# Four of twelve modulation units moved from the first block's layers to the start of the second block

## What is computed

```python
def first_block(...):
    h = x
    for l in range(DEPTH):                      # 2
        h = h + hybrid_mixer(rmsnorm(h, norm_mix[l]), ...)
        h = h + expert_choice_ffn(rmsnorm(h, norm_ffn[l]), ...)
    return rmsnorm(h, norm_final)

def adaln(cvec, w, b):                          # w: 1024 x 6144
    m = jax.nn.silu(cvec) @ w + b
    return [t[..., None, :] for t in jnp.split(m, 6, axis=-1)]

def second_block(x, c, ctx, c_ctx, ...):
    x = x + sincos_2d(...)
    sh1, sc1, gt1, sh2, sc2, gt2 = adaln(c, ada_w[l], ada_b[l])
    csh1, csc1, cgt1, csh2, csc2, cgt2 = adaln(c_ctx, ada_w[l], ada_b[l])
    ...                                         # the context's states use csh1 and csc1
    hx = modulate(rms_norm(x, norm1_g[l]), sh1, sc1)
    x_mix = token_mixer(hx @ w_in[l], ...)
    x = x + gt1 * x_mix
    x = x + gt2 * hier_moe(modulate(rms_norm(x, norm2_g[l]), sh2, sc2), ...)
```

## Time and profile before

| | us |
|---|---|
| median of 3 runs | 2249.55 |
| lowest, highest | 2248.14, 2252.38 |
| the profiled execution | 2247.0 |
| its span, first to last instruction | 2245.2 |
| PE busy in it | 1932.7 |
| DVE, ACT busy | 660.6, 553.6 |
| moved by DMA | 748.76 MB, mean 333 GB/s |

### The profile page before, as it was taken

The page is one execution under the profiler, slowest core; times in us unless marked ns, Lnnn a source line. Parts: engine busy times, 40 slices in busy tenths (PEclk is TensorE's granted clock), DMA queues, the critical chain, the costliest instruction groups (busy, mean ns, idle before and its releaser), DMA issues.

```text
span 2245.2 us, 29187 instructions
## 1 busy us (share of the span) xinstructions
PE 1932.7 (86%) x12802; PEld 1136.0 (51%) x12802; DVE 660.6 (29%) x1074; ACT 553.6 (25%) x849; POOL 0.2 (0%) x4
## 2 busy tenths in 40 slices
PE   7989998777777998998898988879999988888886
PEld 7977932121221897893223433338889732222222
DVE  3467510000000447750150111036657400000001
ACT  3457310000000345630111221023444311010101
POOL 0000000000000000000000000000000000000000
PEclk9999999999999999998999999999999999999999
DMA  9722799999999963379999999983423999999996
GB/s 363 272 100 99 303 389 422 421 421 422 422 421 420 365 237 122 114 309 376 421 418 413 417 417 417 421 321 113 150 95 135 381 421 422 422 422 422 422 421 273
DMA packets 153247, 748.76 MB, mean 333 GB/s; under 512 B 6064, under 2 KB 18608, under 8 KB 78768
## 3 DMA queue, kind: packets, MB, share of 16 engines
q1 hardware_dynamic: 153136, 747.11, 82.9%
HBM read 746.04 MB, written 1.05 MB: 333 GB/s over the span
## 4 chain that ended last, share of the span: by engine, by line
PE 47%; DMA 34%; SPq 9%; ACT 4%; DVE 4%; issue 2%; DVEq 0%; ACTq 0%
PE bank L724 19%; DMA ring<-w_expert_up 12%; DMA ring<-w_expert_down 11%; SPq L2813 9%; PE bank L790 8%; DMA ring<-moe_w_down 6%; PE bank L727 5%; DMA ring<-w_expert_gate 4%; PE bank L820 4%; PE bank L831 1%; PE bank L751 1%; PE bank L974 1%; PE bank L994 1%; DMA ring<-ada_w 1%; PE bank L735 1%
## 5 line engine op out<-in xcount | busy, mean ns | idle before, releaser
L790 PE MATMUL bank<-ring,arena 128*32 128x512 f32 x2560 | 513.3, 600 | 101.6 <-DMA ring<-w_expert_up 52.0
L820 PE MATMUL bank<-ring,arena 128*32 128x512 f32 x1280 | 284.9, 606 | 81.6 <-DMA ring<-w_expert_down 61.5
L790 PEld LDWEIGHTS bank<-ring,arena 128*32 128x32 f32 x2560 | 127.2, 110 | 444.2 <-issue 267.9
L724 PE MATMUL bank<-arena_parts,ring_parts 128*128 128x256 f32 x1376 | 314.5, 284 | 2.4 <-DVE ring_parts L2458 1.6
L724 PEld LDWEIGHTS bank<-arena_parts,ring_parts 128*128 128x128 f32 x1376 | 233.5, 189 | 11.8 <-issue 3.1
L820 PEld LDWEIGHTS bank<-ring,arena 128*32 128x32 f32 x1280 | 67.9, 111 | 287.4 <-issue 153.5
L1519 ACT ACTIVATE arena<-bank 128x512 f32<-128x512 f32 (+1 forms) x150 | 76.0, 536 | 509.7 <-PE bank L806 244.4
L2040 DVE TENSOR_TENSOR arena<-arena,bank 128x512 f32<-128x512 f32 x24 | 15.8, 686 | 591.2 <-PE bank L790 591.2
L724 PE MATMUL bank<-ring_parts 128*128 128x256 f32 x768 | 151.1, 287 | 11.7 <-DVE ring_parts L2458 5.3
L724 PE MATMUL bank<-hnT_parts,ring_parts 128*128 128x256 f32 x544 | 154.3, 284 | 0.0
L724 PEld LDWEIGHTS bank<-ring_parts 128*128 128x128 f32 x768 | 123.8, 191 | 14.7 <-issue 5.2
(11 more groups left out here) (353 smaller groups left out, 2399.4 us busy)
## 6 DMA issues: line engine op xcount, KB each, us to landing
ring<-w_expert_down SPq DMA_DIRECT2D x64, 2048.0 KB, 26.1
ring<-w_expert_up SPq DMA_DIRECT2D x60, 2048.0 KB, 25.0
ring<-w_expert_gate SPq DMA_DIRECT2D x56, 2048.0 KB, 23.4
ring<-w_in SPq DMA_DIRECT2D x34, 2048.0 KB, 10.9
ring<-moe_w_up SPq DMA_DIRECT2D x24, 2048.0 KB, 29.4
ring<-moe_w_gate SPq DMA_DIRECT2D x20, 2048.0 KB, 32.5
ring<-moe_w_down SPq DMA_DIRECT2D x16, 2048.0 KB, 33.0
arena<-moe_w_down SPq DMA_DIRECT2D x16, 2048.0 KB, 32.4
```

The costliest lines, as they stand in the source:

```text
L724: last = pe.matmul(out[:, n * S:(n + 1) * S], w[:, k, n * P:(n + 1) * P], x[:, k, :], start=first, stop=final)
L790: last = pe.matmul(banks[bank0 + f][32 * e:32 * e + 32, :], x_slots[:, c, 32 * e:32 * e + 32], w[:, k, i, f * 512:(f + 1) * 512], start=c ...
L820: last = pe.matmul(banks[4 + d][32 * e:32 * e + 32, :], hidT[:, f, 32 * e:32 * e + 32], w[:, k, i, d * 512:(d + 1) * 512], start=f == 0, s ...
```

## The change

In each layer the head has four ada units now (`ADA_UNITS = 4`), whose columns are still counted by six (`ADA_SPLIT`). The two that are left out (layer 0: units 4 and 5 of 12, layer 1: 10 and 11, the halves of both gates) form `ADA_LATE`. They are loaded at the passage to the second block, in slots 1 and 2, behind the first `w_in_2` unit and ahead of the second and third. TensorE takes two of them between the sums of squares of `f norm` and `x norm`, and two behind `x norm` in place of the filler; the loads of the latter two wait for the former two. ScalarE copies the four results between its second and third weight split, TensorE turns them behind the first projection, VectorE adds the bias after its third weight split.

In the layers, slots 4 and 5 are free earlier: units 8 and 9 of tile 0 are loaded behind units 1 and 2 (`TILE_ORDER`), as soon as `w_branch_a` has been used, and unit 7 moves ahead of 5 and 6. The slots of all units of tile 0 stay as they are. The second block's counts of loads (`RING_LOADS`, `late_before`) follow, and the position table lies 256 columns lower, because the kept ada values are read longer.

```diff
-ADA_UNITS = 6
+ADA_SPLIT = 6
+ADA_UNITS = 4
+ADA_LATE = [layer * ADA_SPLIT + n for layer in range(LAYERS) for n in range(ADA_UNITS, ADA_SPLIT)]
...
+TILE_ORDER = (1, 2, 8, 9, 3, 4, 7, 5, 6)
...
-HEAD_ORDER = [0, 18, 19, 1, 2, 20, 3, 21] + list(range(4, 18)) + [22, 23]
+HEAD_ORDER = [0, 18, 19, 1, 2, 20, 3, 21] + list(range(4, 18))
...
                 token_rows(1)
                 token_rows(3)
-                for n in range(ADA_HEAD, ADA_UNITS):
-                    ada_unit(n)
...
                 def other_slots():
-                    ada_cols("ada 5", take(6, "dve", "ada 5 cols"), ada_rows_late, ADA_UNITS - ADA_HEAD)
...
             for j in range(4):
                 sum_squares_part("f norm", hn3, j, norm_bank, "f squares")
+            late_bank = take(5, "act", "ada late")
+
+            def ada_late(n):
+
+                at = 1 + n % 2
+                pe.wait_ge(unit_loaded[at], (RING_LOADS[at] + 1 + n // 2) * 16)
+                ada_products(late_bank, at, n).then_inc(pe_done, pe_p.mark(f"ada late {n}"))
+
+            ada_late(0)
+            ada_late(1)
             norm_bank = take(7, "act", "x norm root")
             for j in range(4):
                 sum_squares_part("x norm", hn3, j, norm_bank, "x squares")
-            idle_products(banks[4], 16)
+            ada_late(2)
+            ada_late(3)
...
             for n in range(6):
                 job2(HY0 + n, to_dve(f"hy {n}"), hx_high, hn_low, ready=None if n else hx_ready)
+                if n == 0:
+                    ada_cols("ada late", take(4, "dve", "ada late cols"), ada_rows_late, len(ADA_LATE))
...
-            for i in range(1, 8):
+            high2(1)
+            act.wait_ge(pe_done, pe_at(f"ada late {len(ADA_LATE) - 1}"))
+            act.activation(ada_rows_late, banks[5][:], ACT.Copy).then_inc(act_done, act_p.mark("ada late"))
+            for i in range(2, 8):
                 high2(i)
...
                 sp.wait_ge(pe_done, pe_at(f"o win {WIN_HEADS // 2 - 1}", loops))
-                for u in range(1, RING + SPARE):
+                for u in TILE_ORDER:
                     if u == 7:
                         sp.wait_ge(dve_done, dve_at("yb 3", loops))
                     load_tile_unit(0, u)
...
             for i in range(UNITS2_HEAD):
-                if i < HEAD_SLOTS:
-                    sp.wait_ge(pe_done, pe_at(unit_step(STREAMS[LAYERS - 1][i - RING][0])))
+                if i == 0:
+                    sp.wait_ge(pe_done, pe_at(unit_step(STREAMS[LAYERS - 1][-RING][0])))
+                elif i < HEAD_SLOTS:
+                    sp.wait_ge(pe_done, pe_at(f"ada late {i + 1}"))
...
+                if i == 0:
+                    for n, unit in enumerate(ADA_LATE):
+                        at = 1 + n % 2
+                        step = unit_step(STREAMS[LAYERS - 1][at - RING][0]) if n < 2 else f"ada late {n - 2}"
+                        sp.wait_ge(pe_done, pe_at(step))
+                        load_cols(at, io["ada_w_2"], 512 * unit)
```

More of the change, by code:

```diff
@@ L143, in loads @@
             held[at] = (layer, unit)
-    assert count[:RING] == [RING_LOADS] * RING
-    return nth, prior
-NTH_LOAD, PRIOR = loads()
+    return nth, prior, count
+NTH_LOAD, PRIOR, RING_LOADS = loads()
 def unit_step(unit):
@@ L931, in shift_turned, with ada_cols, ada_products @@
                 last.then_inc(pe_done, pe_p.mark("shift cols"))
+            def ada_cols(step, out, of, n_units):
+                pe.wait_ge(act_done, act_at(step, loops))
+                for n in range(n_units):
+                    last = pe.transpose(out[:, n * P:(n + 1) * P], of[:, n * P:(n + 1) * P], ident)
+                last.then_inc(pe_done, pe_p.mark(f"{step} cols"))
+            def ada_products(bank, at, n):
+                w = slot(at).rearrange("p (k n) -> p k n", k=DC)
+                for k in range(DC):
+                    for b in range(4):
+                        last = pe.matmul(bank[32 * b:32 * b + 32, n * P:(n + 1) * P], c_pairs[:, 2 * k:2 * k + 32],
+                                         w[:, k, b * P:(b + 1) * P], start=k == 0, stop=k == DC - 1)
+                return last
             background = {
@@ L1055, in ada_unit @@
                     u = 18 + n
-                    if n % 4 == 0:
-                        ada_banks[n // 4] = take(7, "act", f"ada {min(n + 3, ADA_UNITS - 1)}")
+                    if n == 0:
+                        ada_banks[0] = take(7, "act", f"ada {ADA_UNITS - 1}")
                     if layer == 0 and n == 0:
@@ L1060, in ada_unit @@
                     unit_ready(("head", u), layer)
[L1061 to L1065, removed]
+                    last = ada_products(ada_banks[0], HEAD_AT[u] % RING, n)
                     last.then_inc(pe_done, pe_p.mark(f"ada {n}", unit_done(u)))
@@ L1073, in _ @@
                     job(i, hn_high, hn_low, hn_ready if i == 0 else None)
[L1075 to L1081, removed]
+                ada_cols("ada 3", to_dve("ada 3 cols"), ada_rows, ADA_UNITS)
                 pe.wait_ge(dve_done, dve_at("k_win", loops))
@@ L1823, in high2 @@
                 unit = JOBS2[i][0]
[L1824 removed]
+                act.wait_ge(*head2_loaded(unit))
                 if i >= 2:
@@ L2309, in ada_cols @@
                        .then_inc(dve_done, dve_p.mark(f"{step} cols"))
-                kept = 4 * ADA_UNITS * layer
-                ada_cols("ada 3", bank_v(), ada_raw[:, kept:kept + 4 * ADA_HEAD, :])
+                kept = 4 * ADA_SPLIT * layer
+                ada_cols("ada 3", bank_v(), ada_raw[:, kept:kept + 4 * ADA_UNITS, :])
                 pairs = WIN_HEADS // 2
@@ L2432, in _ @@
                 diagonal("gate diag", gate_diag, topv)
-                ada_cols("ada 5", banks[6], ada_raw[:, kept + 4 * ADA_HEAD:kept + 4 * ADA_UNITS, :])
                 dve.wait_ge(pe_done, pe_at("slot tokens", loops))
@@ L2512, in _ @@
                 low2(j + 2)
+                if j == 0:
+                    late = 4 * ADA_UNITS
+                    n = 4 * ADA_SPLIT - late
+                    dve.wait_ge(pe_done, pe_at("ada late cols"))
+                    dve.tensor_tensor(ada_by_layer[:, :, late:], banks[4][:].rearrange("p (l n x) -> p l n x", l=LAYERS, n=n)[:, :, :, 0:2],
+                                      ada_bias[:, :, late:].broadcast_to([P, LAYERS, n, 2]), ALU.add)\
+                       .then_inc(dve_done, dve_p.mark("ada late cols"))
                 if j == 3:
```

37 lines of the change are left out of this document (19 added, 18 removed).

## The result

| | median us | runs | against the kernel before |
|---|---|---|---|
| before | 2247.58 | 21 | |
| changed | 2252.22 | 21 | 1.0018, 95% interval 1.0011 to 1.0024 |
| changed, measured again | 2251.81 | 9 | 1.0024, 1.0014 to 1.0034 |

The change costs about 4 us (0.18%, interval 2.5 to 5.4 us). That is a little under the 0.2% which the prediction took as the least that one measurement can tell, but both intervals lie above 1, and the two measurements agree. The prediction was +5.35 us, 2254.9.

What follows compares the result with a forecast made beforehand. Some stages are bound by loads, others by TensorE, whose freed buffers set when DMA saturates. Terms -0.75 + 0.5 + 3.0 + 0.9 + 1.7 = +5.35 us, added to 2249.55, give 2254.9 us; range 2249 to 2261 us (8 in 10).

Steps and rivals of the forecast that it cites:

- Bytes worth 0: Layers: two fewer 2 MB loads each save 0 us, since TensorE freeing buffers sets later loads; other bound 9.96 us a layer.
- Rival B: Layers: DMA's backlog sets the saturated stretch's start, so each layer ends 9.96 us earlier, 2235.2 us; chance 0.08.
- The pair's products cost 0 and save 0: Layers, before the first gather: the two ada units' 4.36 and 3.70 us hide behind VectorE's top-k; removal saves 0.
- +0.5 us of clock: Layers, gather and first expert units: TensorE's clock change after the longer wait, both layers together; bounds -1.7 and +2.6 us.
- Second sum of squares behind unit 2, +3.0: Start of second block: the sum queues behind late unit 2 on TensorE, ending at 1509.9 instead of 1506.9 us.
- Units 3 and 4 hidden with 1.2 us to spare: Start of second block: both finish by 1517 us, before a first projection that may start up to 1518.2 at no cost.
- Clock in the passage, +1.7: Start of second block: one low-clock stretch of 3.4 us costs half of itself; bounds 0 and 5 us.
- (1): Sign, layers: loads 10, 11, 12 keep their distance after the first gather, DMA share near 0 ahead of load 10.
- (2): Sign, layers: TensorE waits over 4 us for VectorE ahead of the first gather.
- (3): Sign, passage: second sum of squares ends 3 to 5 us later after the layer's last load, unit 2 right ahead.
- (4): Sign, passage: TensorE's wait for unit 4's load ends before the last normalised tokens; otherwise units 3 and 4's cover was too thin.
- (5): Sign, second block: the rest of it keeps the same length to 1 us.

Runs made afterwards that it cites:

- short_8_9: Kernel before, with only a sixteenth of units 8 and 9 of each layer's first tile loaded; 1.0003 (0.9993 to 1.0014).
- late_8_9: Changed kernel plus 64 unread products per layer at the pair's old place, units 8 and 9 loaded last in old order; 1.0008, against 1.0007 loaded early.
- short_18_19: Kernel before, with only a sixteenth of units 18 and 19 of each layer's first tile loaded; 0.9939, -13.7 us by the ratio.
- no_pair: Kernel before, all loads kept, each of a layer's two late ada units doing 4 of its 32 products; 1.0016, +3.6 us.
- layers_alone: Changed kernel's layers with the four late units left out, passage's filler and load order as before; 1.0017 and, repeated, 1.0013 against the kernel before.

## What the prediction had right, and which step failed

The time was in its range and 0.12% under its point. That is in part luck: two errors offset each other, the layers (forecast -0.25 us, measured +3.3) and the passage (forecast +5.6, by the traces +3.4). And 2.0 of the 2.7 us between forecast and time come from the kernel before, which measured 2247.58 us beside the changed one and not the 2249.55 to which the forecast was added.

- *Bytes worth 0*: right, and shown, by `short_8_9` and `late_8_9`. Rival B (2235.2 us) is out. Load 10, which the prediction held to have queued behind 8 and 9, goes out 6.93 us after the first product with picked tokens in `before` and in `short_8_9` alike, when TensorE ends the first expert unit. The gap ahead of DMA's saturated stretch was made wider at no cost and closed for no gain (share 0.49 and 0.92 above). The Trainium skill, Perfetto Trace Analysis, section "Optimization Strategy", reads a repeated gap on the engine to be saturated as a possible lack of buffers; no run here adds buffers, so whether more of them would pay is not shown. `short_18_19` shows that the same bytes count once DMA sets the pace.
- *The pair's products cost 0 and save 0*: the step that failed. They were called hidden behind the top-k, which they are, and their removal was to cost +0.5 us of clock. `no_pair` measured +3.6 us (1.6 to 5.6), `layers_alone` +3.8 and +2.9 with 0.75 of transposes saved. The term of +0.5 us was mis-sized by a factor of 7 to 8; its upper bound of +2.6 us, for the first layer alone, was nearer. The mechanism was seen, but its price was taken from a few rows of one execution, and so it comes out small (+0.7 us by the third column above); only many executions show the whole. The prediction also set the second layer aside as "at the low clock in this place already". That holds for both profiles that have the pair (its gather took 3.40 and 3.48 us), but with filler it took 2.02 in three of five, so there was something to lose or gain there. The Trainium skill, TensorE: Matmul & The Clock Gate, section "What's actually happening", has the throttled state as the default that activity releases; the runs agree in direction, and the weight that the prediction gave it was too small.
- *Second sum of squares behind unit 2, +3.0*: right. It ended 25.39 us after the last expert unit's landing in place of 22.18, +3.2.
- *Units 3 and 4 hidden with 1.2 us to spare*: wrong by 1.0 us. The last projection start that costs nothing was worked out as 1518.2 and it was 1519.25. Unit 1 met the low clock (3.40 us, not 1.85), so load 3 went out at 1502.82, not 1501.0; load 4 went out at 1506.44 while it was still under way and took 10.88 us. The unit landed at 1517.32, not by 1515.
- *Clock in the passage, +1.7*: two units were slow (3.40 and 3.16 us against 1.95), but both in waits; through the cover of units 3 and 4 they cost the 1.0 us above. The second sum ran at full clock, 3.72 us. The transposes cost 0.44 us on the chain in place of 0.9. In these two profiles 3.2 + 1.0 + 0.44 = 4.6 us accounts for the passage: the first six projections end 69.32 us after the last expert unit's landing in place of 64.80, and w_out's loading goes out 4.3 us later. Over all profiles it is the +3.4 above, where +5.6 was forecast.
- *The signs that the prediction named.* (1) Load 12 and the first wait for a load kept their distance from the gather to 0.2 us; load 10 went out 2.2 us later against it, since gather and first unit took that much longer, at no cost. (2) The wait is 4.57 and 4.58 us (4.6 forecast). (3) +3.2 us. (4) See above: the margin was too thin. (5) From w_out's loading to the last expert unit's landing the second block took 498.57 us, and 498.58 before.

## What to carry to other kernels

TensorE's work that hides in a wait may not be free to remove: here its granted clock around the bare wait was 0.75 to 0.82, and 0.85 to 0.93 where the wait was filled. Before moving such work away, leave products that nobody reads in its place, or measure the kernel with the work left out and everything else kept. Bytes were worth their time here only where DMA's queue, not a freed buffer, set when transfers land; cut the same bytes in two places to find out which holds. Work that moves into a passage is best spread over its waits one unit at a time, with loads that do not wait for each other, and not put in a queue ahead of the step that the passage is waiting for: the same four units cost +3.4 us in one order and nothing measurable in the other.

## What was not expected of the hardware

- About 3 us less work of TensorE per layer made the program 3.6 us slower (1.0016), and 128 products that nobody reads (64 in each layer) made three versions 2.5 to 7 us faster.
- The granted clock of a whole execution differs from run to run (0.972 to 0.987 over all kernels here, and within 12 executions of `layers_alone` 0.972 to 0.980), and the time with it: within kernels, 0.01 of mean clock went with 5.6 us.
- Two loads of 2 MB (1502.82 and 1506.44 us in the passage), of which the first met only the end of another load (landed at 1504.38) and the second was issued 3.6 us after it, took 9.2 and 10.9 us, where one alone takes 8.0; a load of 128 KB took 2.1 us (`short_8_9`).
